# Layer 1's memory K/V projection moved into the chunk attention of a two-layer encoder

## The reference

```python
def chunk_attention(h, w_qkv, w_out, q_g, k_g, rel_bias):   # 16 heads of 64
    q, k = rms_norm(qkv[:, :, 0], q_g), rms_norm(qkv[:, :, 1], k_g)
    s = einsum('bqhd,bkhd->bhqk', q_c, k_c) * scale + bias
    p = softmax(s);  o = einsum('bhqk,bkhd->bqhd', p, v_c)
    return o @ w_out

def memory_cross_attention(h, mem_n, w_q, w_kv, w_out, q_g, k_g):   # 4 heads of 256
    q = rms_norm((h @ w_q).reshape(bsz, seq, XA_HEADS, XA_HEAD_DIM), q_g)
    kv = (mem_n @ w_kv).reshape(bsz, n_mem, 2, XA_HEADS, XA_HEAD_DIM)
    k, v = rms_norm(kv[:, :, 0], k_g), kv[:, :, 1]
    ...
    return o @ w_out
```

## Time and profile before

| | us |
|---|---|
| runs, median of 3 | 1744.21 (1743.7 to 1746.51) |
| span of the profiled execution | 1737.0 |
| PE busy | 1649.4 (95%) |
| DVE busy | 776.2 (45%) |
| ACT busy | 622.6 (36%) |
| POOL busy | 228.3 (13%) |

### The profile page before, as it was taken

How to read it: one execution, slowest core, us unless ns; L and a number is a source line. 1 busy time by engine, 2 the same in 40 slices (tenths; PEclk the granted TensorE clock), 3 DMA queues, 4 the chain that set the end, 5 groups by cost and what they waited for, 6 DMA issues and landing times.

```text
span 1737.0 us, 22605 instructions
## 1 busy us (share of the span) xinstructions
PE 1649.4 (95%) x9358; PEld 1345.0 (77%) x9358; DVE 776.2 (45%) x1011; ACT 622.6 (36%) x1006; POOL 228.3 (13%) x305
## 2 busy tenths in 40 slices
PE   5989989999999999999999997899999999999999
PEld 4778788777768788888888885478776878888887
DVE  4668345453534444442234437835343454444222
ACT  6543333353524322221114335634452432222110
POOL 3853134010000211110000000000000021111000
PEclk9999999999999999999999998999999999999999
DMA  6611012134112333332223221214311233333221
GB/s 208 124 49 50 25 52 75 49 130 137 49 49 73 97 97 97 97 97 97 97 97 98 97 97 37 86 49 145 122 49 49 73 97 97 97 97 97 97 97 73
DMA packets 146801, 151.85 MB, mean 87 GB/s; under 512 B 8864, under 2 KB 109344, under 8 KB 146592
## 3 DMA queue, kind: packets, MB, share of 16 engines
q1 hardware_dynamic: 146720, 150.69, 28.2%
HBM read 147.53 MB, written 3.15 MB: 87 GB/s over the span
## 4 chain that ended last, share of the span: by engine, by line
PE 87%; DVE 7%; ACT 3%; issue 2%; DMA 0%; SPq 0%; POOL 0%; DVEq 0%; ACTq 0%
PE ps L325 24%; PE ps L327 24%; PE ps L326 24%; PE ps L1640 2%; PE ps L1617 1%; PE ps L1996 1%; DVE sb L602 1%; PE ps L956 1%; DVE w_lo_ab L297 1%; DVE sb L2066 1%; ACT w_hi L293 1%; PE ps L1234 1%; PE ps L417 1%; ACT sb L2038 1%; PE ps L1245 1%
## 5 line engine op out<-in xcount | busy, mean ns | idle before, releaser
L325 PE MATMUL ps<-h_hi,w_hi 128*128 128x512 f32 x864 | 337.4, 390 | 4.2 <-DVE w_lo L1810 3.9
L326 PE MATMUL ps<-h_lo,w_hi 128*128 128x512 f32 x864 | 336.2, 389 | 0.0
L297 DVE TENSOR_TENSOR w_lo<-raw,w_hi 128x2048 fp32r<-128x2048 f32 x70 | 160.4, 2292 | 389.8 <-ACT w_hi L293 389.8
L293 ACT ACTIVATE w_hi<-raw 128x2048 fp32r<-128x2048 f32 x84 | 160.7, 1914 | 430.3 <-PE ps L327 429.7
L327 PE MATMUL ps<-h_hi,w_lo 128*128 128x512 f32 x704 | 273.9, 389 | 0.0
L325 PEld LDWEIGHTS ps<-h_hi,w_hi 128*128 128x128 f32 x864 | 162.2, 188 | 38.5 <-issue 5.2
L326 PEld LDWEIGHTS ps<-h_lo,w_hi 128*128 128x128 f32 x864 | 162.2, 188 | 33.3
L1810 DVE TENSOR_TENSOR w_lo<-raw,w_hi 128x2048 fp32r<-128x2048 f32 x44 | 138.1, 3138 | 53.5 <-ACT w_hi L1792 53.5
L327 PEld LDWEIGHTS ps<-h_hi,w_lo 128*128 128x128 f32 x704 | 132.1, 188 | 27.7
L1792 ACT ACTIVATE w_hi<-raw 128x2048 fp32r<-128x2048 f32 x44 | 84.3, 1916 | 160.9 <-PE ps L327 160.9
L325 PE MATMUL ps<-w_hi,a_hi 128*128 128x512 f32 x352 | 137.3, 390 | 1.7 <-DVE up L1808 1.7
(11 more groups left out here) (370 smaller groups left out, 2667.8 us busy)
## 6 DMA issues: line engine op xcount, KB each, us to landing
raw<-in_f_w_gate SPq DMA_DIRECT2D x44, 512.0 KB, 4.0
raw<-in_f_w_up SPq DMA_DIRECT2D x44, 512.0 KB, 5.2
raw<-in_f_w_down SPq DMA_DIRECT2D x44, 512.0 KB, 4.2
raw<-in_xa_w_kv SPq DMA_DIRECT2D x16, 1024.0 KB, 5.0
raw<-in_c_w_qkv SPq DMA_DIRECT2D x12, 1024.0 KB, 5.1
raw<-in_ab_w_in SPq DMA_DIRECT2D x10, 1024.0 KB, 5.8
raw<-in_xa_w_q SPq DMA_DIRECT2D x8, 1024.0 KB, 5.0
raw<-in_xa_w_out SPq DMA_DIRECT2D x8, 1024.0 KB, 5.0
```

The source lines that it names most:

```text
L293: a.activation(w_hi[:, n % 2, :], raw[n % 2], ACT.Copy).then_inc(sem("w_hi"), 1)
L297: v.tensor_tensor(w_lo(n)[:, n % 2, :], raw[n % 2], w_hi[:, n % 2, :].bitcast(F32), ALU.subtract).then_inc(sem("w_lo"), 1)
L325: pe.matmul(out, a[0], b[0], start=start, stop=False)
L326: pe.matmul(out, a[0], b[1], start=False, stop=False)
```

## The change

PE: the 192 matmuls of layer 1's K/V projection leave their place behind the output projection. They are cut into 8 groups (4 weight panels by 2 tiles of memory rows) of 8 products. Group 0 stands between the scores of round 1 and the first transposes; group m+1 stands in round m (0 to 6), one product behind each group of transposes. They write PSUM bank 6, and the transposes are left with two banks instead of three. The 32 transposes of x are spread: 16 go into the output projection's second half, 16 into the query projection's first.

POOL: it splits the memory (1 cast and 1 subtraction of 2048 elements a partition), and six of the eight weight pieces (`KV1_POOL`: each as two halves of a cast and a subtraction of 1024), between the masks. ACT and DVE split the first two pieces where they split the output projection's first two before. ACT copies each group's result out of bank 6. The K rows' norm is taken behind the attention from SBUF.

SP: the pieces `kv10_0` to `kv13_1` are loaded between the bias tiles, and the output projection's pieces behind all of them. ACT splits both pieces of `cao0` ahead of the last round's copies, DVE ahead of the last `out_lo`.

The diff's core (offsets of buffers and layer indices are left out):

```diff
             g.tensor_tensor(memT, mem_T[0].bitcast(F32), mem_T[1].bitcast(F32), ALU.add).then_inc(sem("mem_kept"), 1)
 
-        def mem_split_act(a):
-            a.wait_ge(sem("mem_kept"), after("mem_kept", 1))
-            a.wait_ge(sem("c_o"), CH // 2)
-            a.activation(mem_T1[0], memT, ACT.Copy).then_inc(sem("mem_hi"), 1)
-
-        def mem_split_dve(v):
-            v.wait_ge(sem("mem_hi"), 1)
-            v.tensor_tensor(mem_T1[1], memT, mem_T1[0].bitcast(F32), ALU.subtract).then_inc(sem("mem_lo"), 1)
+        def mem_split_pool(g):
+            g.wait_ge(sem("mem_kept"), after("mem_kept", 1))
+            g.wait_ge(sem("ca_turned"), 8)
+            link(g, g.tensor_copy(mem_T1[0], memT), "s5_pool")
+            g.tensor_tensor(mem_T1[1], memT, mem_T1[0].bitcast(F32), ALU.subtract).then_inc(sem("mem_lo"), 1)
+        KV1_POOL = ["kv11_0", "kv11_1", "kv12_0", "kv12_1", "kv13_0", "kv13_1"]
+        def kv1_piece_pool(g, name):
+            n = where[name]
+            g.wait_ge(slot_landed[n % 2], landed[n])
+            g.wait_ge(panel_used, n - 1)
+            g.wait_ge(sem("w_hi"), nth(n))
+            g.wait_ge(sem("w_lo"), nth(n))
+            for half, hi_done, lo_done in ((0, "k1_hi", "k1_lo"), (1, "w_hi", "w_lo")):
+                c = slice(half * PIECE // 2, (half + 1) * PIECE // 2)
+                g.tensor_copy(w_hi[:, n % 2, c], raw[n % 2][:, c]).then_inc(sem(hi_done), 1)
+                g.wait_ge(sem(hi_done), KV1_POOL.index(name) + 1 if half == 0 else nth(n) + 1)
+                g.tensor_tensor(w_lo(n)[:, n % 2, c], raw[n % 2][:, c], w_hi[:, n % 2, c].bitcast(F32), ALU.subtract).then_inc(sem(lo_done), 1)
+        def kv1_fill_pe(pe, g, k):
+            j, i, kh = g // 2, g % 2, k // 4
+            name = f"kv1{j}_{kh}"
+            if g == 0 and k == 0:
+                pe.wait_ge(sem("mem_lo"), 1)
+            if k == 0:
+                pe.wait_ge(sem("k1_out"), g)
+            if k % 4 == 0 and i == 0 and name in KV1_POOL:
+                pe.wait_ge(sem("k1_lo"), KV1_POOL.index(name) + 1)
+            elif k % 2 == 0 and i == 0:
+                pe.wait_ge(sem("w_lo"), nth(where[name]) + 1)
+            w = tuple(v[:, where[name] % 2, :].rearrange("p (k n) -> p k n", k=4) for v in (w_hi, w_lo(where[name])))
+            ins = product(pe, ps[:, 6, :], of(mem_T1, k, slice(i * P, (i + 1) * P)), of(w, k % 4), k == 0, k == KT - 1)
+            if i == 1 and k % 4 == 3:
+                ins.then_inc(panel_used, 1)
+            elif k == KT - 1:
+                ins.then_inc(sem("k1_mm"), 1)
+        def kv1_out_act(a, g):
+            j, i = g // 2, g % 2
+            if i == 0:
+                a.wait_ge(sem("k1_mm"), j + 1)
+            else:
+                a.wait_ge(panel_used, where[f"kv1{j}_1"] + 1)
+            dst = xk_rows[1] if j < 2 else xv[1]
+            a.activation(dst[:, i, j % 2 * 512:(j % 2 + 1) * 512], ps[:, 6, :], ACT.Copy).then_inc(sem("k1_out"), 1)
+
...
                 rows_pe(pe, t, f"xq{l}{j}", hT, TT, 4 * j,
                         ready=(lambda k: ready_T(pe, f"x{l}", k)) if j == 0 else None,
-                        bank_free=lambda i: ready_T(pe, f"x{l}", 4 * j + i))
+                        bank_free=lambda i: ready_T(pe, f"x{l}", 4 * j + i),
+                        mid=(lambda: turn_rows_pe(pe, f"x{l}", 1, "co_x")) if l == 1 and j == 0 else None)
             kv_turn_pe(pe, l)
 
             for k in range(KT):
...
@@ -1978,13 +2045,15 @@
             for n in range(8):
                 s, e = n // 2, n % 2
                 g = 8 * m + n
-                if g >= 3:
-                    pe.wait_ge(sem(COPY[(g - 3) % 8][0]), 4 * ((g - 3) // 8) + COPY[(g - 3) % 8][1])
+                if g >= 2:
+                    pe.wait_ge(sem(COPY[(g - 2) % 8][0]), 4 * ((g - 2) // 8) + COPY[(g - 2) % 8][1])
                 for i in range(s, TT):
                     if s == 0:
                         pe.wait_ge(sem(RESCALE[i][0]), after(RESCALE[i][0], RESCALE[i][1] * (2 * m + e) + RESCALE[i][2]))
-                    ins = pe.transpose(ps[:, 4 + g % 3, i * P:(i + 1) * P], p_c(m, e, i)[:, s * P:(s + 1) * P], ident)
+                    ins = pe.transpose(ps[:, 4 + g % 2, i * P:(i + 1) * P], p_c(m, e, i)[:, s * P:(s + 1) * P], ident)
                 ins.then_inc(sem("c_tr"), 1)
+                if m + 1 < CH // 2:
+                    kv1_fill_pe(pe, m + 1, n)
 
         def ca_values_pe(pe, m):
...
@@ -2017,6 +2086,8 @@
 
             ca_scores_pe(pe, 0)
             ca_scores_pe(pe, 1)
+            for k in range(KT):
+                kv1_fill_pe(pe, 0, k)
             for m in range(CH // 2):
                 ca_turn_p_pe(pe, m)
                 if m + 2 < CH // 2:
...
             for m in range(CH // 2):
                 if m + 1 < CH // 2:
                     a.wait_ge(sem("c_max"), m + 2)
+                else:
+                    a.wait_ge(sem("w_hi"), nth(where["cao0_0"]))
+                    split["a"] = where["cao0_0"]
+                    pieces_hi(a, "cao0_1")
                 for e in range(2):
                     for j in range(4):
                         if m + 1 < CH // 2:
@@ -2051,6 +2127,8 @@
                         n = 4 * e + j
                         if COPY[n][0] == "c_pa":
                             ca_copy(a, m, n)
+                if m + 1 < CH // 2:
+                    kv1_out_act(a, m + 1)
                 a.wait_ge(sem("c_o"), m + 1)
                 a.activation(c_oT[0][:, m, :].rearrange("p (i n) -> p i n", i=TT),
...
+            v.wait_ge(sem("w_lo"), nth(where["cao0_0"]))
+            split["v"] = where["cao0_0"]
+            pieces_lo(v, "cao0_1")
             out_lo(CH // 2 - 1)
 
...
-            for m in range(CH // 2):
-                mask(m)
-            g.wait_ge(sem("c_mask"), after("c_mask", CH))
+            mask(0)
+            mask(1)
+            g.wait_ge(sem("c_mask"), after("c_mask", 4))
+            mem_split_pool(g)
+            g.wait_ge(sem("mem_lo"), 1)
+            mask(2)
+            mask(3)
+            for p, name in enumerate(KV1_POOL):
+                g.wait_ge(sem("c_mask"), after("c_mask", 2 * min(p + 4, CH // 2)))
+                kv1_piece_pool(g, name)
+                if p + 4 < CH // 2:
+                    g.wait_ge(sem("w_lo"), nth(where[name]) + 1)
+                    mask(p + 4)
 
 
...
@@ -2152,13 +2243,19 @@
             xres_sp(sp)
             mem_sp(sp)
             load_pieces(sp, "abo1_0", "abo1_1")
-            load_pieces(sp, "kv00_0", "ca5_1")
+            load_pieces(sp, "kv00_0", "kv10_1")
             for h in range(4):
                 ca_sp(sp, h)
-            load_pieces(sp, "cao0_0", "cao0_1")
-            for h in range(4, CH):
+            load_pieces(sp, "kv11_0", "kv11_1")
+            for h in range(4, 12):
                 ca_sp(sp, h)
-            load_pieces(sp, "cao1_0", f"dn1_{FT // 2 - 1}")
+            load_pieces(sp, "kv12_0", "kv12_0")
+            for h in (12, 13):
+                ca_sp(sp, h)
+            load_pieces(sp, "kv12_1", "kv12_1")
+            for h in (14, 15):
+                ca_sp(sp, h)
+            load_pieces(sp, "kv13_0", f"dn1_{FT // 2 - 1}")
             for i in range(TT):
                 sp.wait_ge(sem("d1_x"), after("d1_x", TT + i + 1))
...
@@ -2211,18 +2308,18 @@
             pe.wait_ge(sem("mo_x"), after("mo_x", 8))
             norm_pe(pe, "m", mem_x, mem_x)
             for l in range(DEPTH):
-                if l == 1:
-                    pe.wait_ge(sem("mem_lo"), 1)
-                kv_pe(pe, l)
-
-                pe.wait_ge(sem(f"kv{l}_k"), after(f"kv{l}_k", 4))
-                pe.wait_ge(sem(f"kv{l}_v"), after(f"kv{l}_v", 4))
-                for half in range(2):
-                    turn_rows_pe(pe, f"x{l}", half, "co_x" if l else "mo_x")
+                if l == 0:
+                    kv_pe(pe, l)
+                    pe.wait_ge(sem(f"kv{l}_k"), after(f"kv{l}_k", 4))
+                    pe.wait_ge(sem(f"kv{l}_v"), after(f"kv{l}_v", 4))
+                    for half in range(2):
+                        turn_rows_pe(pe, f"x{l}", half, "mo_x")
+                else:
+                    pe.wait_ge(sem("k1_out"), 8)
                 xq_pe(pe, l)
                 xa_pe(pe, l)
 
-                split_outproj_pe(pe, f"xo{l}", xo[l], oT, ready=lambda k: pe.wait_ge(sem(f"xa{l}_ov"), after(f"xa{l}_ov", k + 1)), between=lambda: turn_rows_pe(pe, f"f{l}", 0, f"xo{l}_x"))
+                split_outproj_pe(pe, f"xo{l}", xo[l], oT[l], ready=lambda k: pe.wait_ge(sem(f"xa{l}_ov"), after(f"xa{l}_ov", k + 1)), between=lambda: turn_rows_pe(pe, f"f{l}", 0, f"xo{l}_x"))
                 ffn_up_pe(pe, l)
                 ffn_down_pe(pe, l)
                 if l == 0:
@@ -2230,8 +2327,7 @@
                     ca_turn_pe(pe)
                     ca_pe(pe)
                     pe.wait_ge(sem("c_ol"), CH // 2)
-                    split_outproj_pe(pe, "co", cao, c_oT)
-                    pe.wait_ge(sem("co_x"), after("co_x", 8))
```

(48 more changed lines are left out.)

78 lines of the change are left out of this document (49 added, 29 removed).

## The result

The changed kernel takes 1756.15 us (median of 4 runs, 1754.47 to 1757.49), the kernel before in the same comparison 1744.49 (4 runs, 1743.7 to 1746.51). The ratio is 1.0066, with a 95% interval of 1.0053 to 1.008: **slower by 11.7 us, 0.66%**. Forecast were 1757 us and +12.7. The profiled execution of the changed kernel has a span of 1755.7 us (run time 1757.49), the one of before 1737.0.

What follows compares the result with a forecast made beforehand. PE was taken to bound the kernel, with 16.5 us free in the attention. Terms 28 + 4 + 5.5 + 10 + 12 - 46.8 = +12.7 us on 1744.2 gave 1757 us; range 1741 to 1766, about 0.78.

Steps and rivals of the forecast that it cites:

- What goes: Between first output product and first query product: 94.0 us shrinks by 46.8, after 43.8 and 3.4 that stay.
- Seven rounds with products: Attention rounds: PE alone sets 13.7 us a round, 4.0 longer than before, +28 us over seven.
- The start: Start of attention: group 0 delays first transposes 3.1 us, DVE's subtraction waits for POOL's memory split, +1; together +4.
- The end: Last round: ACT's and DVE's weight splits delay transposes and the last low part, plus slow clock; together +5.5 us.
- Late pieces: Rounds 1 and 3: PE waits for POOL's weight pieces, 2.5 and 7.5 us; together +10, bounds 0 and 14.
- The port: Rounds 0 and 5: DVE's SBUF-to-SBUF scalings and POOL's instructions shut each other out; +12 us, bounds 0 and 30.
- the full wait: DVE's scalings beside POOL: each waits out the POOL instruction it meets, 1.0 or 2.4 us; four end 6.8 late.
- the second rival: Attention: either scalings don't meet POOL (+1.7, 1746 us) or weight pieces are in time (+2.7, 1747); chance 0.15.
- The rounds named as bare: Rounds 2, 4 and 6: 13.7 us from scores to scores, PE idle under 1 us in each.
- those named as disturbed: Rounds 1 and 3, PE waiting for POOL's low part (some 7 us in 3); round 5, transposes waiting for a scaling.
- The first rival: Whole change works as meant: pieces in time, scalings don't meet POOL; -10.2 us, 1734 us; chance 0.18.

Runs made afterwards that it cites:

- the kernel with the slower scalings: Changed kernel with the attention's scalings also writing row sums, which takes them out of the fast form: 1745.83 us, ratio 1.0006 to the kernel before.
- the kernel with all three edits: Changed kernel with row-sum scalings for odd rounds' probabilities, ACT's and DVE's end splits moved, weight pieces loaded and split earlier: 1728.91 us, ratio 0.9913 to the kernel before.

## Why the prediction was right, step by step

- **What goes** (-46.8): 46.9. The two streams and the spread transposes cost what their rows of before said.
- **Seven rounds with products** (+28): an undisturbed round is 13.5, not 13.7, so six rounds give 6 x 3.85 = 23.1, and round 0's turning part took 3.5 us more than before; 26.6 in all. The turning part was put at 8.3 us and took 7.9, so between groups of transposes a product adds 0.04 us to its matmuls, not 0.09. The rest was put 0.2 too short: scores were to shrink to 3.1 us, but the last pair waits 0.69 us for its sums as before, and they take 3.3. That two banks cost nothing behind a product is what the trace shows (one wait of 0.58 us for a copy in all seven rounds, in the round in which the negation took 1.28). The sentence beside it, that without the cover the turning part would be what it is now, was wrong: it would be 1.6 us a round longer.
- **The start** (+4): the first transposes come 3.1 us later against the first scores. The subtraction beside POOL cost 0.9, as put. Group 0 was oversized: its 24 matmuls stand in one row and take 5.6 us, since there is no change of kind between them.
- **The end** (+5.5): 15.8 us from the values of round 6 to the first output product, 10.3 before: +5.5. Run with the splits elsewhere, 5.2 of them went.
- **Late pieces** (+10, bounds 0 and 14): 2.5 for `kv11_1` and 7.8 for `kv12_1`. The chain sums, bias tile, mask, split was read from three rows of before, and for `kv12_1` it came out to 0.3 us. The 2.5 was taken and not added up: the prediction's own times (first half at 6.9, the second 3.5 later, product 6 due near 6.4) give 4.0. The trace has 2.5 because the slow clock of round 0 put 2.6 us, not 0.7, between the end of the sums and the transposes. Without it, in the kernel with the slower scalings, that round is 3.6 us over an undisturbed one. That this term was hit is partly luck.
- **The port** (+12, bounds 0 and 30): 4.5 in round 0 and 9.2 in round 5, 13.6 in all. Here the step was least sure, since no row of before had a scaling beside a long POOL instruction. The choice of the full wait, by the copy on 64 elements (POOL's row at 363.34 beside the other one is an addition, not the subtraction it is called there, which changes nothing), decided between slower and no change that can be told from noise (+1.7 in the second rival). The mechanism was right, scalings and POOL's instructions in turns; the longest scaling took 2.5, put at up to 2.8. Its sizes were less so: four scalings end 5.3 and 5.9 us late, put at 6.8. In round 0 the 4.5 is right by two errors: the scores' last pair had 2.4 us to spare and not 1 to 2, so that the wait grew by 2.8 only, and a slow clock that was priced for round 5 alone gave 1.7. In round 5 the +6 holds 1.2 us from the negation ahead of the scalings, which the prediction does not have, and the slow clock was undersized, 2.6 against 1.5.

Six terms, none off by more than 1.7 us, and their errors partly cancel: +12.3 in the profile for +12.7. So the causes and the order of their sizes were foreseen, and the hit within 1 us is in part luck. The span of 1749.7 that the prediction also names was 1755.7, since it was built on the quick profiled execution of before; the median was built on the differences and is not touched by it. The rounds named as bare (13.7 us, PE idle under 1 us) and those named as disturbed are the ones in the trace, except that the port's cost in round 0 and the late piece in round 1 stand in one interval between scores. The first rival failed on the late pieces, which were said against it, and on the port. That it was a real possibility is shown by the kernel with all three edits, at 1728.9.

What the prediction did not see: how near the gain was. None of the three causes belongs to moving the products. Each was an order on another engine, and they are worth 27 us together, more than twice what the change lost.

## What to carry to other kernels

Before work is given to GpSimd because it is idle, look what VectorE does SBUF to SBUF at that moment: put the work beside VectorE's instructions that read PSUM, or take those that wait out of their fast form where someone waits for them. Take all of them: here a negation of 8 elements was left, and it cost up to 1.2 us where it met GpSimd. A stream moved into the waits of a bound engine gains only the waits that it truly fills; here a round had 2.6 us of them for 6.2 us of products. And where two delays lie on one chain, move the first before pricing the second: the later meeting may not take place.

## What the runs showed of the hardware that I had not expected

- A VectorE scaling with a row sum costs little more than one without: 0.75 us for 512 elements and 1.9 us for four of 512 to 128 with their accumulator reads, against 1.27 us for the four in the fast form. Beside a GpSimd instruction it keeps that time, where a single one of the fast form took up to 2.59 us (2.54 in the changed kernel).
- Short instructions are held up too: a `tensor_scalar` on 8 elements, 0.17 us alone, took 1.40 us beside a GpSimd subtraction and 0.98 beside a cast.
- A GpSimd cast of 1024 elements a partition took 1.04 us and a subtraction 2.36. Against the scalings these became 1.17 and 2.44 at most: nearly all of the waiting is on VectorE's side.
- Of five rounds with like waits of 2.8 to 3.0 us on PE, four lost 1.5 to 1.8 us more than the wait (13.3 to 13.6 us against 11.8 in the fifth), and the one shown stood at 0.50, 1.2 of 2.4 GHz, behind it, where the fifth kept 1.00. A wait and its clock are two terms, and the second is not certain.
